# Gate rows moved from ahead of the attention into the recurrence, with a reordered first stage and a first output tile taken by K-steps

## What is computed

```python
mod = jax.nn.silu(cvec) @ p["w_ada"] + p["b_ada"]
shift, scale, gate = jnp.split(mod, 3, axis=-1)
h = _rmsnorm(x, p["norm_g"]) * (1.0 + scale[:, None, :]) + shift[:, None, :]
z = h @ p["w_in"]
hy_z, hy_g, rw_z, rw_g, da_q, da_k, da_v, da_g, mg = jnp.split(z, IN_SPLITS, axis=-1)
y_a = _hyena_branch(hy_z, hy_g, p)                    # long convolution by FFT
y_b, s_f, s_b = _rwkv_branch(rw_z, rw_g, p, s0_f, s0_b)  # two scans, one each way
y_c, k_c, v_c = _diff_branch(da_q, da_k, da_v, da_g, p, lam_init, ctx_kv)  # uses lambda
merged = (g_a * (y_a @ p["w_br"][0]) + g_b * (y_b @ p["w_br"][1])
          + g_c * (y_c @ p["w_br"][2]))
out = merged.astype(x.dtype) @ p["w_out"]
x_new = x + (gate[:, None, :] * out).astype(x.dtype)
```

## Time and profile before

| | us |
|---|---|
| median of 3 runs | 2689.14 (2686.93 to 2691.93) |
| the profiled execution | 2685.29 |
| its span, first to last instruction | 2683.4 |
| TensorE busy | 2482.6 (93%) |
| VectorE busy | 1282.2 (48%) |
| ScalarE busy | 846.4 (32%) |
| GpSimd busy | 630.6 (23%) |
| mean granted clock of TensorE | 0.966 of full |

### The profile page before, as it was taken

How to read it: one execution, slowest core, us unless ns; L and a number is a source line. 1 busy time by engine, 2 the same in 40 slices (tenths; PEclk the granted TensorE clock), 3 DMA queues, 4 the chain that set the end, 5 groups by cost and what they waited for, 6 DMA issues and landing times. The chain is left out here.

```text
span 2683.4 us, 58871 instructions
## 1 busy us (share of the span) xinstructions
PE 2482.6 (93%) x25008; PEld 1702.4 (63%) x25008; DVE 1282.2 (48%) x2290; ACT 846.4 (32%) x1628; POOL 630.6 (23%) x594
## 2 busy tenths in 40 slices
PE   6999997899899999999999999979999999999999
PEld 3557664566666767677555576646666667667765
DVE  5763427463737364432157624275545464644321
ACT  3221425542434242222032224165343333322220
POOL 1232210212222222333011332202121313133320
PEclk8999998999999999999989999999999999999999
DMA  7112130101001010322541111301010101013132
GB/s 266 63 36 71 48 102 32 40 19 35 28 28 36 28 36 29 110 68 67 195 148 48 44 63 55 126 0 41 27 36 28 36 20 43 20 44 110 63 110 71
DMA packets 41994, 165.65 MB, mean 62 GB/s; under 512 B 5200, under 2 KB 5200, under 8 KB 40208
## 3 DMA queue, kind: packets, MB, share of 16 engines
q1 hardware_dynamic: 35856, 131.09, 14.3%
q0 software_dynamic: 5888, 30.87, 3.1%
HBM read 149.88 MB, written 12.06 MB: 60 GB/s over the span
## 5 line engine op out<-in xcount | busy, mean ns | idle before, releaser
L776 PE MATMUL ps<-scr 32*32 32x32 f32 (+8 forms) x17800 | 700.3, 229 | 73.6 <-issue 24.2
L776 PEld LDWEIGHTS ps<-scr 32*32 32x32 f32 (+5 forms) x17800 | 539.4, 124 | 270.2 <-issue 224.0
L776 PE MATMUL ps<-h,ring 128*128 128x320 f32 x1280 | 391.0, 451 | 9.5 <-ACT h L1715 4.7
L828 PE MATMUL ps<-x,ring 128*128 128x320 f32 x1152 | 354.4, 449 | 21.0 <-DVE scr L2197 17.0
L776 PEld LDWEIGHTS ps<-h,ring 128*128 128x128 f32 x1280 | 246.9, 197 | 117.6 <-issue 26.7
L828 PEld LDWEIGHTS ps<-x,ring 128*128 128x128 f32 x1152 | 218.9, 195 | 119.1 <-issue 42.1
L2197 DVE TENSOR_TENSOR scr<-ps,scr 128x320 f32<-128x320 f32 x168 | 81.7, 490 | 425.5 <-PE ps L776 270.6
L607 POOL TENSOR_TENSOR ring<-ring,sums 128x512 f32<-128x512 f32 x64 | 90.5, 1414 | 701.8 <-PE ps L776 612.8
L1666 ACT ACTIVATE scr<-ps 128x320 f32<-128x320 f32 x168 | 72.8, 435 | 319.7 <-PE ps L776 225.8
L828 PE MATMUL ps<-h,ring 128*128 128x320 f32 x576 | 171.4, 438 | 0.8 <-issue 0.8
L776 PE MATMUL ps<-h,sums 128*128 128x320 f32 x576 | 170.6, 436 | 0.9 <-issue 0.6
(11 more groups left out here) (317 smaller groups left out, 3115.4 us busy)
## 6 DMA issues: line engine op xcount, KB each, us to landing
ring<-in_w SPq DMA_DIRECT2D x240, 512.0 KB, 3.5
spill<-x POOLq DMA_DIRECT2D x8, 640.0 KB, 3.6
scr<-spill POOLq DMA_DIRECT2D x2, 2560.0 KB, 10.8
x<-in_x SPq DMA_DIRECT2D x1, 2560.0 KB, 16.7
yc<-in_win POOLq DMA_DIRECT2D x2, 1280.0 KB, 7.6
x<-in_x POOLq DMA_DIRECT2D x2, 1280.0 KB, 9.6
out_y<-x POOLq DMA_DIRECT2D x8, 320.0 KB, 6.6
x<-out_y POOLq DMA_DIRECT2D x2, 1280.0 KB, 10.2
```

What stands on the lines that cost most here:

```text
L776: return nc.tensor.matmul(out, lhsT, rhs, start=start, stop=stop)
L828: return nc.tensor.matmul(out, lhsT, rhs, start=False, stop=stop, skip_group_check=True)
```

## The change

Five things change.

1. Slots: the gate slots leave their places around the ag pairs. Behind the two early slots of each j of the recurrence now stand two of them.
2. TensorE: gate_rows(j) computes two blocks at a time into its own columns of PSUM (bank 3), behind parts[5] of direction 1. For even j ScalarE copies the half sum (into the par columns of lambda's vectors, free by then), for odd j VectorE adds the other half. The rows are turned behind product4 of rk/rv in j = 2 and behind the pair m10/m11; ScalarE copies the columns out, and VectorE adds the bias and halves ahead of the output's eviction. GpSimd makes the sums of the next rk/rv behind its diagonal copies. The load of the next layer's parameters waits for the first output tile too.
3. Attention: lambda is finished ahead of the ag pairs. Even units of the scores use the upper banks and odd ones the lower, and pairs_evicted(PAIR_WL) stands between scores(0) and scores(1).
4. First stage: windowed(1) goes behind the add of product7 in j = 2; turn_p(0) goes between product3 and product4 of pair 3, its copy ahead of that step's taps; two adds of hy0 go ahead of the last four spectrum products of f = 1.
5. Output: tile 0 goes to banks 2 and 3, and each of its K-steps waits for its own merged tile.

```diff
 for _j in range(0, JT, 2):
-    ORDER += [("z", f"ag{_j}"), ("z", f"ag{_j + 1}")] + GATE[2 * _j:2 * _j + 4]
+    ORDER += [("z", f"ag{_j}"), ("z", f"ag{_j + 1}")]
 ORDER += [("lora",), ("z", "wl"), ("z", "al")]
 for _j in range(JT):
-    ORDER += [("z", f"{_n}{_j}") for _n in ("rk", "rv", "rr", "rg")] + [("z", EARLY[2 * _j]), ("z", EARLY[2 * _j + 1])]
+    ORDER += [("z", f"{_n}{_j}") for _n in ("rk", "rv", "rr", "rg")] + [("z", EARLY[2 * _j]), ("z", EARLY[2 * _j + 1])] + GATE[2 * _j:2 * _j + 2]
...
-        gaterow = [pdT[:, i * 256:(i + 1) * 256] for i in range(2)]
+        gaterow = par[:, PCOL["lq1"][0]:PCOL["lq1"][0] + 256]
...
+        def score_bank(u):
+            return 1536 * (1 - u % 2)
...
+        gate_row_bank, gate_bank = ps[:, 1664:1920], ps[:, 1920:1936]
+        def out_bank(j):
+            return wide(4 + 2 * (j % 2) if j else 2)
...
                     if d == 0:
                         early_last_sum(j)
-                    else:
-                        sums_of(PAIR_R + 2 * j + 2)
...
                         nc.gpsimd.tensor_copy(t3(TTall, 128)[rows, :, rows], t3(TTc, 32)[rows, :, :]).then_inc(diag_ready, 1)
+                    if d == 1:
+                        pool.wait_ge(diag_ready, 4 * g + 4)
+                        sums_of(PAIR_R + 2 * j + 2)
...
                     pool.wait_ge(merged_ready, KD)
+                    pool.wait_ge(out_read, 1)
...
-                last_three(3)
+                product7(3)
+                product3(3)
                 turn_p(0)
+                product4(3)
                 turn_p(1)
...
+                first_four(PAIR_AG + 1)
+                last_three(PAIR_AG + 1)
+
                 pe.wait_ge(v_done, JT)
-                for q in range(4):
-                    rows_of_mod(4, q, weights("gate", 0, q))
-                first_four(PAIR_AG + 1)
-                pe.wait_ge(gate_row, 1)
-                turn_row(gate_bank[:, 0:8], gaterow[0])
-                last_three(PAIR_AG + 1)
-                for q in range(4):
-                    rows_of_mod(5, q, weights("gate", 1, q))
-                pe.wait_ge(gate_row, 2)
-                turn_row(gate_bank[:, 8:16], gaterow[1]).then_inc(gate_turned, 1)
-
-                pairs_evicted(PAIR_WL)
...
                 scores(0)
+                pairs_evicted(PAIR_WL)
                 scores(1)
...
+                def gate_rows(j):
+                    n = j // 2
+                    pe.wait_ge(gate_row, j)
+                    for part in range(2):
+                        q = 2 * (j % 2) + part
+                        w = weights("gate", n, q)
+                        for kk in range(2):
+                            k = 2 * q + kk
+                            for half in range(2):
+                                at = 64 * kk + 32 * half
+                                o = kk * 512 + half * 256
+                                i = mm(gate_row_bank[at:at + 32, :], sc[:, 32 * k:32 * k + 32], w[:, o:o + 256], part == 0, part == 1)
+                        i.then_inc(w_used, 1)
+                def turn_gate_row(n):
+                    pe.wait_ge(gate_row, 2 * n + 2)
+                    turn_row(gate_bank[:, 8 * n:8 * n + 8], gaterow).then_inc(gate_turned, 1)
...
                     product4(n)
+                    if j == 2:
+                        turn_gate_row(0)
...
                         early_part(j, *parts[5])
+                        if d == 1:
+                            gate_rows(j)
...
                             last_three(n)
+                            if n == PAIR_M + 1:
+                                turn_gate_row(1)
...
-                pe.wait_ge(merged_ready, KD)
                 pairs_evicted(len(PAIRS))
...
                     for k in range(KD):
-                        i = wide_mm(4 + 2 * (j % 2), w[:, k * 128:(k + 1) * 128], tile(mg, k), k == 0, k == KD - 1)
+                        if j == 0:
+                            pe.wait_ge(merged_ready, k + 1)
+                        for cols in (slice(0, S), slice(S, T)):
+                            i = mm(out_bank(j)[:, cols], w[:, k * 128:(k + 1) * 128], tile(mg, k)[:, cols], k == 0, k == KD - 1)
...
+                    if j == 3:
+                        turned_p(0)
...
                     if j == 2:
                         dve.wait_ge(win_in, l * 16 + 16)
                         windowed(0)
-                        windowed(1)
                     if j == 3:
                         windowed(4)
                     if j:
                         added(j, 7)
+                    if j == 2:
+                        windowed(1)
+                    if j:
                         added(j, 3)
...
                     dve.sem_inc(U_read, 1)
+                    if f == 1:
+                        added(PAIR_HY, 2)
+                        added(PAIR_HY, 7)
...
-                added(PAIR_HY, 2)
-                added(PAIR_HY, 7)
...
+                def gate_row_added(j):
+                    dve.wait_ge(w_used, used(l, ("gate", j // 2, 3)))
+                    dve.wait_ge(gate_row, j)
+                    TTn(gaterow, gate_row_bank, gaterow, ADD).then_inc(gate_row, 1)
...
                     if j >= 1:
                         centred(j - 1)
+                    if j == 2:
+                        gate_row_added(1)
```

More of the change, by code:

```diff
@@ L500, in build @@
         mod_row, row_turned = signal("mod_row"), signal("row_turned")
-        gate_row, gate_turned = signal("gate_row"), signal("gate_turned")
+        gate_row, gate_turned, gate_copied = (signal(n) for n in ("gate_row", "gate_turned", "gate_copied"))
         sq_ready, sq_used, rt_ready = signal("sq_ready"), signal("sq_used"), signal("rt_ready")
@@ L1135, in scores @@
                         pe.wait_ge(e_ready, u - 1)
-                    base = 1536 * (u % 2)
+                    base = score_bank(u)
                     (q0, q1), (k0, k1), (p0, p1) = ([a[64 * m:64 * m + 64] for m, a in enumerate(pair)] for pair in (
@@ L1709, in copy_gate_row, with copy_gates @@
                 def copy_gate_row(n):
-                    act.wait_ge(w_used, used(l, ("gate", n, 3)))
-                    A_(gaterow[n], ps[:, 512 * (4 + n):512 * (4 + n) + 256], ACT.Copy).then_inc(gate_row, 1)
+                    act.wait_ge(w_used, used(l, ("gate", n, 1)))
+                    if n:
+                        act.wait_ge(gate_turned, n)
+                    A_(gaterow, gate_row_bank, ACT.Copy).then_inc(gate_row, 1)
+                def copy_gates(n):
+                    act.wait_ge(gate_turned, n + 1)
+                    A_(dcol("mod", 32 + 8 * n, 8), gate_bank[:, 8 * n:8 * n + 8], ACT.Copy).then_inc(gate_copied, 1)
                 for k in range(KD):
@@ L1752, in _ @@
                     lin(f"hx{j}", u_x[j % 2], pcol("cw1", 8 + j), pcol("cb", 8 + j))
-                for j in range(3):
+                for j in range(1, JT):
                     turned_p(j)
-                turned_p(3)
                 for f in range(NF):
@@ L1817, in turned_v @@
                     act.sem_inc(z_free, 1)
+                act.wait_ge(lam_ready, 1)
+                A_(dcol("ls", 2, 2), dcol("ls", 0, 2), ACT.Exp).then_inc(lam_exp, 1)
                 copies(PAIR_AV + 1)
@@ L1949, in _ @@
                         copied(n, 1)
+                    if j % 2 == 1:
+                        copy_gate_row(j // 2)
                     copied(n, 5)
@@ L1963, in _ @@
                     copied(n, 1)
+                    if j == 2:
+                        copy_gates(0)
                     act.wait_ge(k_ready, j + 1)
@@ L2074, in _ @@
                         copied(m, 5)
+                        if n == 4:
+                            copy_gates(1)
                         if n == 0:
@@ L2386, in _ @@
                         rotated(2 * j - 1)
+                dve.wait_ge(lam_exp, 1)
+                link(TTn(dcol("neglam"), dcol("ls", 3), dcol("ls", 2), SUB))
+                link(TTn(dcol("neglam"), dcol("neglam"), pcol("laminit"), SUB))
                 all_added(PAIR_AV + 1)
@@ L2391, in _ @@
                     silu_of(f"ag{j}", tile(gsb, j), zc[j % 2])
-                dve.wait_ge(gate_turned, 1)
-                link(TTn(m3[:, 16:24, :], gate_bank.rearrange("p (a n) -> p a n", n=2), pcol("bada", 16, 8).unsqueeze(2).to_broadcast([128, 8, 2]), ADD))
-                do(TS(dcol("gate", 0, 16), mod[:, 32:48], 0.5, None, MUL))
-                dve.wait_ge(lam_exp, 1)
-                link(TTn(dcol("neglam"), dcol("ls", 3), dcol("ls", 2), SUB))
-                link(TTn(dcol("neglam"), dcol("neglam"), pcol("laminit"), SUB))
                 units = [(hd_, q) for hd_ in range(HEADS) for q in range(NT)]
@@ L2407, in maxima @@
                     dve.wait_ge(s_full1, u + 1)
[L2408 removed]
+                    V.tensor_reduce(st[:, 0:2], t3(ps[:, score_bank(u):score_bank(u) + 2 * MAP1], MAP1)[:, :, 0:w], AX.X, ALU.max, negate=True).then_inc(s_max, 1)
                 def combine(u):
@@ L2687, in _ @@
```

(6 more changed lines are left out.)

9 lines of the change are left out of this document (2 added, 7 removed).

## The result

| | before | after |
|---|---|---|
| median of three runs, us | 2689.14 | 2651.84 (2645.91 to 2654.44) |
| profiled execution, us (span) | 2685.3 (2683.4) | 2645.91 (2644.1) |
| mean granted clock | 0.966 | 0.974 |

The ratio of the runs is 0.9856, 95% interval 0.9832 to 0.988: 37.3 us between the medians, where the prediction had 36.8.

A forecast was written before the change was run, and what follows sets the result against it. TensorE, busy 2482.6 of 2683.4 us, was taken as the bound. 9.2 - 3.4 + 31.1 - 6.8 - 1.6 - 2.0 + 10.3 = 36.8 us gain from the 2689.1 median; predicted 2652 us, range 2641 to 2670.

The forecast's parts named there:

- First stage: Step j = 2: product4 no longer waits for VectorE's adds and runs at full clock; gain 9.2 us, between 0 and 9.8.
- hy0: Transform: earlier adds move TensorE's wait from product4 to the inverse transform, which then runs slowly; loss 3.4 us, 0 to 5.
- Attention's front: From ag0's product4 to the first maximum: without gate rows the stretch falls to 19.6 us; gain 31.1 us, low end 28.
- Rival (c): Attention: something other than TensorE holds the first maximum, only gate-row ring waits go; gain 16.7 us, 2672.4 us; chance 0.06.
- Gate rows in the recurrence: Behind direction 1's last early product: eight visits, 0.85 of 1.07 us each on the path; loss 6.8 us, 0 to 8.6.
- Turns: Gate-row turns: j = 2 bounded by 0.8 us, behind pair m10 no cover; loss 1.6 us, between 0 and 3.2.
- Three loads on end: Recurrence: loads of rv, rr, rg following each other may delay instructions; 0.25 us in each of eight visits, loss 2.0 us.
- above 28.3 us by more than a few: TensorE's issue waits, 28.3 us in the profile before: a rise beyond this was listed as showing the prediction wrong.
- (b): Recurrence: each of eight visits meets a 2.3 us halt from three loads on end; gain 20.4 us, 2668.7 us; chance 0.10.
- (d): Recurrence: rv's late load delays GpSimd's sums, TensorE stands at product5; slower than before from 24.3 us on; chance 0.04.
- Output: First output tile: by K-steps in free banks it starts right behind the last branch product; gain 10.3 us, low end 6.8.

The follow-up runs named there:

- The narrow rows: Changed kernel with gate rows of 64 columns instead of 256, number of matmuls and slots unchanged: 2645.46 us, ratio 0.9824 against the kernel before.
- the sums held: Changed kernel with GpSimd's three early sums waiting until VectorE has turned direction 0's first two blocks: 2629.86 us, ratio 0.9789 against the kernel before.
- everything but the move: Kernel before with only the first stage, hy0 and output edits, gate rows left in the attention's front: 2671.62 us, ratio 0.9936 against the kernel before.
- the gap alone: Changed kernel with gate rows behind direction 0's first products, their slots before the early ones, GpSimd's sums before the diagonal copies: 2640.39 us, ratio 0.9818.
- the sums held as well: Changed kernel with gate rows in direction 0's gap and GpSimd's early sums held until VectorE turned the first two blocks: 2628.54 us, ratio 0.9785.

## Why the prediction was right

- **First stage** (9.2): 4.9 and 5.1 us in the two traces. Its two halves were put slightly wrong: product4 gave 4.3 a layer and not 4.6, the earlier turning 0.5 and not nothing (product3 to transform 7.71 us, before 8.25). The 1.8 us for the slow clock took 3.96 us, which run to the end of the last instruction, against 2.16 from start to start; like with like it is 3.96 - 2.39 = 1.6. The share of the slow clock isn't firm, as its undoing showed.
- **hy0** (-3.4): the wait moved as said, from 2.46 us ahead of product4 to 3.92 ahead of the transform. The cost was 0 in layer 0 and 2.6 in layer 1, inside 0 to 5.
- **Attention's front** (31.1): 16.0 and 14.9 us. The new stretch is 19.72 us in both layers (predicted 19.6), and VectorE's last silu is what the first maximum follows. Rival (c) falls with that. How much of it each part brought (the rows away, the banks of the scores, the place of the eviction wait) no run separates.
- **Gate rows in the recurrence** (-6.8): 19.89 - 19.13 = 0.76 us, eight times 6.1. The narrow rows show that it is their length.
- **Turns** (-1.6): the pair of j = 2 went from 57.5 to 57.6 us, hidden. With the sums held the same pair is at 57.0 beside 56.1: 0.9 once VectorE, its cover, is no longer late. The turn behind the pair m10/m11 costs 0.8 a layer: from the last product there to the next one it is 2396.69 - 2393.73 = 3.0 us, before 2431.33 - 2429.18 = 2.2. Together 1.8.
- **Three loads on end** (-2.0): not borne out. The issue waits are 32.0 us before and 32.5 with the new order of slots; with the old order and the other three edits they are 35.3 (31.6 at L779, 3.7 at L831). The sign "above 28.3 us by more than a few" looked at one of two lines. No ring wait falls into the recurrence, and the sums end at 1919.2 against product5 at 1931.6, 12 us of slack (predicted 9). Rivals (b) and (d) fell with that.
- **Output** (10.3): 5.1 and 5.0 us to the read of tile 0 in the two layers.

These terms sum to 40.4 us without the loads (10.0 - 2.6 + 30.8 - 6.1 - 1.8 + 10.1). The two profiled spans differ by 39.3 and the medians by 37.3, so nothing is missing that these runs could tell from noise. That 36.8 lies so near to 37.3 is luck in part. The 2.0 us charged for loads cost nothing, and the first stage was put 0.8 us too low, hy0's cost 0.8 too high, so the marks stand 3.6 us above the forecast; the medians came out 3.1 below the marks.

The prediction had no term for one thing that the experiments found: it looked at GpSimd only as a queue and never at what its sums do to VectorE beside them. The rows were in the trace of before, too, where 25 of 104 VectorE instructions of 128x127 took 1.35 to 1.43 us instead of 0.34, each beside a GpSimd sum. The move made it slightly worse in one place. The product pairs behind the first visit of layer 0 take 61.1 us instead of 57.5, with product4 waiting 2.67 us and then taking 4.08, and between 60.3 and 61.1 in every kernel that keeps this order of slots and sums; direction 0 right behind it gives back 2.7 (32.7 instead of 35.4).

Sums over the whole recurrence in one trace are weaker evidence than they look. They are 995.0 us before and 1003.3 after, but 1004.6 in the kernel with everything but the move, whose recurrence is that of before.

What stays open is the source of the issue waits. They don't come from the early slot's load. In direction 0, from the first blocks to the read of the side, those above 0.5 us sum to 7 us over the eight visits with the gap alone and to 25 with the sums held as well, with the same loads: they grow there when waits ahead of the dense 32x32 part go. That would fit a limit in how fast instructions arrive, but no run varied that alone. The prediction took all of them for the cost of streaming instructions, but fetches that come late explain at most a part: in the trace of before a fetch of instructions (16 KB in its own DMA queue) lands inside 4 of the 25 waits above 0.5 us, the two longest among them, 8.3 of 28.5 us.

## What to carry to other kernels

Price a moved block by the gap it leaves and the gap it enters, measured between neighbouring marks of one trace: gate rows of 1.07 us cost 0.76 on the solve's chain, and nothing one gap earlier once GpSimd's sums were out of the way. When an engine's instruction is now and then several times its usual length, look at what GpSimd ran beside it; one wait that moved GpSimd's sums was worth 18 us beside the 37 of the whole change. When only the place of a wait changes, ask which of the two batches behind it is hidden, since that one should take the slow clock.

## What the runs showed of the hardware

- The same wait of 2.68 us at the same product was followed by 1.2 GHz in one execution (granted clock 0.53, 3.96 us) and by 2.4 GHz in another (1.00, 2.39 us). Behind a wait of 3.9 us twenty matmuls took 4.14 us in one layer and 7.08 in the other.
- Matmuls into four strips of 32 rows run beside each other: sixteen in 1.07 us, four into one strip in 1.05.
- A VectorE operation of 0.33 us on two SBUF inputs takes 1.3 us beside a GpSimd sum of 1.27.
